# Tensor engine: sample rows' high and low parts as one stationary block in the down products, a 360-column last chunk, and an earlier start of the first up products

## What is computed

```python
mix = jnp.concatenate([o_b, o_a], axis=-1) @ w_out[l]
x = x + rmsnorm(mix, norm_mix_post[l])
f, new_buf = conv_ffn(rmsnorm(x, norm_ffn_pre[l]), conv_buf, w_up[l], conv_w[l], conv_b[l], w_down[l])
x = x + rmsnorm(f, norm_ffn_post[l])

def conv_ffn(xn, buf, w_up, conv_w, conv_b, w_down):
    h = xn @ w_up                                   # 1024 -> 2 * 2816
    hp = jnp.concatenate([buf, h], axis=1)
    c = conv_b + sum(conv_w[j] * hp[:, j:j + L] for j in range(3))
    g, u = jnp.split(c, 2, axis=-1)
    return (jax.nn.silu(g) * u) @ w_down, hp[:, L:]  # 2816 -> 1024
```

## Time and profile before

| | |
|---|---|
| time, median of 3 runs | 1434.85 us (1434.38 to 1435.5) |
| profiled execution, its time | 1435.23 us |
| profiled execution, span from first to last instruction | 1433.5 us |
| PE busy | 1390.9 us, 97% |
| DVE busy | 706.1 us, 49% |
| ACT busy | 464.0 us, 32% |
| POOL busy | 170.4 us, 12% |
| granted TensorE clock, mean | 0.993 |

### The profile page before, as it was taken

How to read it: one execution, slowest core, us unless ns; L and a number is a source line. 1 busy time by engine, 2 the same in 40 slices (tenths; PEclk the granted TensorE clock), 3 DMA queues, 4 the chain that set the end, 5 groups by cost and what they waited for, 6 DMA issues and landing times.

```text
span 1433.5 us, 22554 instructions
## 1 busy us (share of the span) xinstructions
PE 1390.9 (97%) x8818; PEld 1253.6 (87%) x8818; DVE 706.1 (49%) x1068; ACT 464.0 (32%) x779; POOL 170.4 (12%) x321
## 2 busy tenths in 40 slices
PE   7999999989999899999999999999999999999996
PEld 6999999957667688899898989898989898989995
DVE  5333322265666655445636353545454545353647
ACT  5421021065655544334132313132323232323233
POOL 2253000111222221120000000000000000000005
PEclk9999999999999999999999999999999999999998
DMA  7102022175573623132111101111110202020106
GB/s 256 60 30 63 30 96 74 66 211 171 161 223 117 192 87 118 66 96 74 30 59 29 59 29 59 29 48 40 32 55 16 71 15 73 15 73 15 45 23 129
DMA packets 93210, 112.39 MB, mean 78 GB/s; under 512 B 6413, under 2 KB 65206, under 8 KB 93142
## 3 DMA queue, kind: packets, MB, share of 16 engines
q1 hardware_dynamic: 89765, 103.34, 23.0%
q0 software_dynamic: 1136, 4.06, 1.6%
q10 hardware_dynamic: 2240, 4.06, 0.8%
HBM read 96.76 MB, written 14.69 MB: 78 GB/s over the span
## 4 chain that ended last, share of the span: by engine, by line
PE 89%; DVE 3%; issue 2%; ACT 2%; POOL 2%; DMA 1%; SPq 1%; ACTq 0%; DVEq 0%
PE PS L2086 36%; PE PS L2137 18%; PE PS L1821 16%; PE PS L2042 7%; PE PS L2156 2%; PE PS L1914 2%; PE PS L1983 1%; PE PS L1937 1%; PE PS L1882 1%; POOL small L1223 1%; DVE small L1412 1%; PE PS L1889 1%; PE PS L1904 1%; PE PS L1960 1%; PE PS L1807 1%
## 5 line engine op out<-in xcount | busy, mean ns | idle before, releaser
L2086 PE MATMUL PS<-act_hi,wu_hi 128*128 128x364 f32 x1056 | 347.7, 329 | 3.6 <-DVE wu_lo L1597 2.6
L2086 PE MATMUL PS<-act_lo,wu_hi 128*128 128x364 f32 x1056 | 347.7, 329 | 0.0
L2086 PE MATMUL PS<-act_hi,wu_lo 128*128 128x364 f32 x1056 | 347.5, 329 | 0.0
L2086 PEld LDWEIGHTS PS<-act_hi,wu_hi 128*128 128x128 f32 x1056 | 199.2, 189 | 4.3 <-DVE wu_lo L1597 2.7
L2086 PEld LDWEIGHTS PS<-act_lo,wu_hi 128*128 128x128 f32 x1056 | 199.0, 188 | 0.4
L2086 PEld LDWEIGHTS PS<-act_hi,wu_lo 128*128 128x128 f32 x1056 | 199.2, 189 | 0.0
L1649 DVE TENSOR_TENSOR y_acc<-y_acc,PS 128x512 f32<-128x512 f32 x180 | 123.3, 685 | 138.0 <-PE PS L2137 138.0
L2137 PE MATMUL PS<-wd_hi,g_hi 128*128 128x512 f32 x360 | 143.9, 400 | 0.0
L2137 PE MATMUL PS<-wd_hi,g_lo 128*128 128x512 f32 x360 | 142.3, 395 | 0.0
L2137 PE MATMUL PS<-wd_lo,g_hi 128*128 128x512 f32 x360 | 141.9, 394 | 0.0
L1110 ACT CAST g_hi<-conv 128x1088 fp32r<-128x1088 f32 x21 | 23.2, 1103 | 270.7 <-PE PS L2137 219.4
(11 more groups left out here) (254 smaller groups left out, 2335.7 us busy)
## 6 DMA issues: line engine op xcount, KB each, us to landing
wu_raw<-in_w_up_dram SPq DMA_DIRECT2D x44, 512.0 KB, 3.8
kpage<-in_cache_k_dram SPq DMA_DIRECT2D x64, 256.0 KB, 3.0
vpage<-in_cache_v_dram SPq DMA_DIRECT2D x64, 256.0 KB, 3.0
wd_raw<-in_w_down_dram SPq DMA_DIRECT2D x22, 512.0 KB, 5.3
w_raw<-in_w_in_dram SPq DMA_DIRECT2D x20, 512.0 KB, 4.8
wo_raw<-in_w_out_dram SPq DMA_DIRECT2D x8, 512.0 KB, 5.4
x_res<-in_x_prompt_dram SPq DMA_DIRECT2D x8, 512.0 KB, 4.3
out_dram<-x_mid SPq DMA_DIRECT2D x8, 512.0 KB, 2.9
```

The lines of the kernel that those rows point to most:

```text
L2086: mm = nc.tensor.matmul(PS[:, 3 * half + c, 0:CW], a[:, half, k, :], b[:, k, CHUNKS[c]], start=(j == 0), stop=(j == len(parts) - 1))
```

## The change

1. `g_hi` has 64 columns more. The product is cast into columns 64 to 1151; columns 0 to 63 take the sample rows' low part, written by an extra DVE instruction over 64 columns (`gs_lo_ready`). `g_lo` keeps the prompt only. For tile 8 the stationary block is columns 0 to 127 of `g_hi`, 64 low and 64 high parts of the same rows, and it is multiplied by `wd_hi` and by `wd_lo`: 4 matmuls in a group and not 6. The low parts' results gather in rows 64 to 127 of tile 8 of `y_acc`, to which all 128 rows are now added.
2. At the end these rows are moved to partitions 0 to 63 by a DMA on SP's queue (`y_fold`, 256 KB), behind a wait for the sample tile's two adds and ahead of the stores of the states; DVE adds them after the third tile's adds (`fold_sample`). Square, root, scaling and store of the sample tile come as the fourth (`NORM_POS`), and DVE makes two `final_norm` in the seventh step.
3. Chunk 2 is 360 columns wide in all up products, in the input projections u, k and q, and in the last copy.
4. The first up weights of both sides are split ahead of the last out tile's work (`wu_hi_first`, `wu_lo_first`), into the place of `w_out`'s high parts 0 to 3, behind a wait for the last tile's products that read them (`wo_used`). PE makes chunk 1 of the gate side right after the states, then turns tile 7 (into banks 4 and 5, which waits for the sample tile's `y_nrm`), makes chunk 2, turns the sample tile, and makes chunk 1 of the up side before it waits for the sample tile's split. `x2_hi` and `x2_lo` of tile 7 come after the sample tile's scaling.

```diff
-    g_hi = ffn.put("g_hi", [P, 2, NTOK], F32R)
-    g_lo = ffn.put("g_lo", [P, 2, NTOK], F32R)
+    g_hi = ffn.put("g_hi", [P, 2, NS + NTOK], F32R)
+    g_lo = ffn.put("g_lo", [P, 2, SEQ], F32R)
...
+    NORM_POS = [1, 2, 3, 0, 4, 5, 6, 7, 8]
+    y_fold = wd_raw[0:NS, 1, :]
...
         sp.dma_start(x_last, y_out[STEPS - 2]).then_inc(xlast_loaded, 16)
+        sp.wait_ge(ybank_free, YJ * (NIT - 1) + 2 + 2)
+        sp.dma_start(y_fold, y_acc[NS:P, STEPS - 1, :]).then_inc(fold_loaded, 16)
         for j, q in enumerate(STATES_FIRST):
             store_states(j, q)
...
         def wu_hi_first(half):
+            act.wait_ge(wo_used, 1)
...
+            if t == STEPS - 1:
+                wu_hi_first(0)
+                wu_hi_first(1)
             act.wait_ge(y_ready, t + 1)
...
             if t == STEPS - 1:
                 x2_hi(t - 2)
-                x2_hi(t - 1)
-                wu_hi_first(0)
...
-        wu_hi_first(1)
+        x2_hi(STEPS - 2)
         x2_hi(STEPS - 1)
...
             if t == STEPS - 1:
+                wu_lo_first(0)
+                wu_lo_first(1)
                 x2_lo(t - 2)
-                x2_lo(t - 1)
-                wu_lo_first(0)
             dve.wait_ge(yrstd_ready, t + 1)
...
-        wu_lo_first(1)
+        x2_lo(STEPS - 2)
         x2_lo(STEPS - 1)
+        for i in range(2):
+            dve.wait_ge(xmid_stored[i], 16 * ((STEPS + 1 - i) // 2))
...
-                    nc.vector.tensor_tensor(g_lo[:, e, :], conv[:, 1, :], g_hi[:, e, :].bitcast(F32), ALU.subtract).then_inc(g_lo_ready, 1)
+                    nc.vector.tensor_tensor(g_hi[:, e, 0:NS], conv[:, 1, 0:NS], g_hi[:, e, NS:2 * NS].bitcast(F32), ALU.subtract).then_inc(gs_lo_ready, 1)
+                    nc.vector.tensor_tensor(g_lo[:, e, :], conv[:, 1, NS:], g_hi[:, e, 2 * NS:].bitcast(F32), ALU.subtract).then_inc(g_lo_ready, 1)
...
         for t in range(STEPS):
             last_add(t, 0)
-            if t >= 2:
+            if 3 <= t <= 6:
+                final_norm(t - 3)
+            if t >= 6:
                 final_norm(t - 2)
             last_add(t, 1)
+            if t == 2:
+                fold_sample()
...
+            if t == STEPS - 2:
+                pe.wait_ge(ynrm_ready, STEPS)
...
-        pe.wait_ge(xt_lo_ready, 2 * STEPS + 2 * (STEPS - 1))
-        for c in (1, 2):
-            up_chunk(0, c)
+        pe.wait_ge(xt_lo_ready, 2 * STEPS + 2 * (STEPS - 3))
+        up_chunk(0, 1)
+        turn_x2(STEPS - 2)
+        up_chunk(0, 2)
         turn_x2(STEPS - 1)
+        pe.wait_ge(wu_lo_ready, 2)
+        pe.wait_ge(xt_lo_ready, 2 * STEPS + 2 * STEPS - 2)
+        up_chunk(1, 1)
         pe.wait_ge(xt_lo_ready, 2 * STEPS + 2 * STEPS)
...
-                for c in range(1 if first and t == 0 else 3):
+                for c in (0,) if first and t == 0 else (0, 2) if first and t == 1 else range(3):
                     mm = up_chunk(half, c)
...
+        def down_parts(s):
+
+            if s == STEPS - 1:
+                return [(g_hi[:, e, 0:2 * NS], w, e) for e in range(2) for w in (wd_hi, wd_lo)]
+            t = slice(2 * NS + P * s, 2 * NS + P * s + P)
+            return [(g, w, e) for e in range(2)
+                    for g, w in ((g_hi[:, e, t], wd_hi), (g_hi[:, e, t], wd_lo), (g_lo[:, e, P * s:P * s + P], wd_hi))]
```

More of the change, by code:

```diff
@@ L396, in _program, with kept @@
     KEPT = [slice(CW * c, min(CW * (c + 1), NTOK)) for c in range(3)]
+    def kept(c):
+        return KEPT[c].stop - KEPT[c].start
     jobs = []
@@ L1645, in add_down @@
             t, half = n // 2, n % 2
-            r = rows(t)
             dve.wait_ge(down_ready, base + n + 1)
-            dst = y_acc[0:r, t, 512 * half:512 * half + 512]
-            nc.vector.tensor_tensor(dst, dst, PS[0:r, 6 + half, :], ALU.add).then_inc(ybank_free, 1)
+            dst = y_acc[:, t, 512 * half:512 * half + 512]
+            nc.vector.tensor_tensor(dst, dst, PS[:, 6 + half, :], ALU.add).then_inc(ybank_free, 1)
         def ffn_dve(i, first, last):
@@ L1750, in last_add, with fold_sample @@
         def last_add(t, half):
-            s = LAST_TILES[t]
-            r, n = rows(s), 2 * t + half
+            s, n = LAST_TILES[t], 2 * t + half
             dve.wait_ge(down_ready, YJ * (NIT - 1) + n + 1)
-            dst = y_acc[0:r, s, 512 * half:512 * half + 512]
-            nc.vector.tensor_tensor(dst, dst, PS[0:r, LAST_BANK[t % 4] + half, :], ALU.add).then_inc(ybank_free, 1)
+            dst = y_acc[:, s, 512 * half:512 * half + 512]
+            nc.vector.tensor_tensor(dst, dst, PS[:, LAST_BANK[t % 4] + half, :], ALU.add).then_inc(ybank_free, 1)
+        def fold_sample():
+            dve.wait_ge(fold_loaded, 16)
+            dve.wait_ge(ybank_free, YJ * (NIT - 1) + 2 + 2)
+            dst = y_acc[0:NS, STEPS - 1, :]
+            nc.vector.tensor_tensor(dst, dst, y_fold, ALU.add).then_inc(fold_ready, 1)
         def final_norm(t, cs=slice(0, D)):
-            s = LAST_TILES[t]
+            s = LAST_TILES[NORM_POS[t]]
             r = rows(s)
@@ L1814, in project @@
                 else:
-                    out = PS[:, bank_of[n], 0:CW]
-                    pairs = [(w[:, g % 2, k, P * f:P * f + P], a[:, k, CHUNKS[c]]) for k in range(KD)
+                    out = PS[:, bank_of[n], 0:kept(c)]
+                    pairs = [(w[:, g % 2, k, P * f:P * f + P], a[:, k, KEPT[c]]) for k in range(KD)
                              for w, a in ((w_hi, act_hi), (w_hi, act_lo), (w_lo, act_hi))]
@@ L2058, in _ @@
                 mm = out_products(t, k, j == 0, j == KD - 1)
+                if t == STEPS - 1 and k in (1, 3):
+                    mm.then_inc(wo_used, 1)
             mm.then_inc(y_ready, 1)
@@ L2085, in up_chunk @@
             for j, (a, b, k) in enumerate(parts):
[L2086 removed]
+                mm = nc.tensor.matmul(PS[:, 3 * half + c, 0:kept(c)], a[:, half, k, :], b[:, k, KEPT[c]],
                                       start=(j == 0), stop=(j == len(parts) - 1))
@@ L2134, in down_share @@
                 pe.wait_ge(ybank_free, YJ * i + n + 1)
-                parts = [(g, w, e) for e in range(2) for g, w in ((g_hi, wd_hi), (g_hi, wd_lo), (g_lo, wd_hi))]
+                parts = down_parts(t)
                 for j, (g, w, e) in enumerate(parts):
-                    mm = nc.tensor.matmul(PS[:, 6 + half, :], g[:, e, wide(t)], w[:, e, 512 * half:512 * half + 512],
+                    mm = nc.tensor.matmul(PS[:, 6 + half, :], g, w[:, e, 512 * half:512 * half + 512],
                                           start=(j == 0), stop=(j == len(parts) - 1))
@@ L2153, in _ @@
                     pe.wait_ge(ybank_free, YJ * (NIT - 1) + 2 + 2 * (t - 4) + half + 1)
-                parts = [(g, w, e) for e in range(2) for g, w in ((g_hi, wd_hi), (g_hi, wd_lo), (g_lo, wd_hi))]
+                parts = down_parts(s)
                 for j, (g, w, e) in enumerate(parts):
-                    mm = nc.tensor.matmul(PS[:, LAST_BANK[t % 4] + half, :], g[:, e, wide(s)], w[:, e, 512 * half:512 * half + 512],
+                    mm = nc.tensor.matmul(PS[:, LAST_BANK[t % 4] + half, :], g, w[:, e, 512 * half:512 * half + 512],
                                           start=(j == 0), stop=(j == len(parts) - 1))
```

54 lines of the change are left out of this document (36 added, 18 removed).

## The result

The changed kernel takes **1421.75 us** (median of 4 runs, 1420.87 to 1422.97); the kernel before, on the same chip, 1434.84 (1434.38 to 1435.5, 4 runs). The ratio is 0.9909, 95% interval 0.9892 to 0.9926: 13.1 us less. That is 2.1 us above the forecast of 1419.6 and inside the wide range of 1417.0 to 1423.5, but 0.25 outside the forecast's own range of 1418.0 to 1421.5. The profiled execution took 1421.63 us, with a span of 1419.9.

A forecast was written before the change was run, and what follows sets the result against it. PE's own time was taken as the bound in the FFN. Shares 8.4, width 2.4 and transition 5.0 less closing stage 0.5 gave 15.3 us saved, so 1419.6 us; own range 1418.0 to 1421.5, wide range 1417.0 to 1423.5.

The forecast's parts named there:

- What bounds the kernel: FFN: PE's own time is the bound, 89% of the span; a matmul taken out counts in full unless something else comes last.
- 1. Shares: Ten down shares: four fewer matmuls each, 0.94 us less about 0.1 for a bank wait; net 8.4 us, between 7.0 and 9.4.
- Rival C: Down shares: the bank wait takes half of each share's gain, giving 1424 us; chance 0.06.
- rival E: Down shares: the new short PE wait brings the clock down, 18 us in ten shares, giving 1437.4 us; chance 0.01.
- 2. Width: Last chunks of up products and projections: 1344 matmuls with 4 columns less, 1.8 ns each; 2.4 us, range 0 to 2.5.
- Rival B: Last chunks: 360 columns cost what 364 do, giving 1422 us; chance 0.10.
- 3. Transition: First up products: 2.7 us idle, 1.8 of low clock, 1.15 idle go, 0.6 wait comes; gain 5.0, range 3.2 to 5.6.
- Rival A: Transition gives less: PE still idles, or the clock falls again at turns or the new wait; 1423 us, chance 0.12.
- 4. Closing stage: End of kernel: POOL's late root delays DVE's fifth scaling; end 0.5 us later though PE is 0.85 sooner, range -0.8 to +1.5.
- The sum: Whole kernel: 8.4 + 2.4 + 5.0 - 0.5 = 15.3 us saved, giving 1419.6 from the median of 1434.85.

The follow-up runs named there:

- e2: Kernel before with only the last chunk of up products and projections at 360 columns: 1432.65 us, ratio 0.9987.
- e1: Kernel before with only the new shares and closing stage, old width and old transition order: 1427.37 us, ratio 0.9947.
- e11: Kernel before plus unread identity transposes in PE's idle stretches ahead of the out products, no part of the change: 1434.53 us, ratio 1.0.
- e3: Kernel before with only the early split of the up weights and new order of turns and first up products: 1429.88 us, ratio 0.9965.
- e6: Changed kernel with POOL's closing root as one instruction, constant 1e-6 left out: 1420.75 us, ratio 0.9896.
- e4: The whole changed kernel once more, unaltered, in a later set of runs against the kernel before: 1420.17 us, ratio 0.99.
- e9: The whole changed kernel, unaltered, in another later set of runs against the kernel before: 1420.24 us, ratio 0.99.
- The fillers: Changed kernel plus identity transposes nobody reads, meant for PE's idle stretches ahead of and among the first out products: 1419.78 us, ratio 0.9898.
- e7: Changed kernel without the fold, sample tile first in the closing order, sample rows lacking their low parts' products: 1418.98 us in one execution.
- e12: Changed kernel without the fold and with the closing stage of before, now timed: 1418.40 us, ratio 0.9882.

## Why the prediction was right, and where it was not

**What bounds the kernel**: right. The share and the up products have moved by what their matmuls cost, and nothing else came last there.

**1. Shares**: right. Forecast 0.94 less 0.1 us each; measured 25.32 - 24.49 = 0.83. The cost is where it was laid out, at the second of the two short groups, whose load waits for the last add. Timelines of weight load and PE in after:

```profile
850.41 0.19 PEld L2195 LDWEIGHTS PS<-wd_hi,g_hi 128*128 128x128 f32 x1 [0.28 <-DVE y_acc L1677]
```

```profile
850.41 0.50 PE L2195 MATMUL PS<-wd_hi,g_hi 128*128 128x512 f32 x1
850.75 0.40 PE L2195 MATMUL PS<-wd_lo,g_hi 128*128 128x512 f32 x1
```

The step from one matmul to the next is 0.34 and not 0.234: 0.11 us, between the bounds of 0 and 0.24. Rival C (half the gain) is out, and so is the slower rival E: the nine iterations of after with that wait show no row of lower clock. What the Trainium skill ("TensorE: Matmul & The Clock Gate", A second HAM failure mode) tells of such small waits between PSUM banks, that the clock swings with them, did not happen here: this wait is 0.11 us of PE.

**2. Width**: the mechanism right, the size within 0.5 us. An up block of 288 has 96 narrower matmuls and takes 0.20 us less: 2.1 ns each, where 1.8 was forecast. Alone (e2) the part gave 1.95 us for a forecast of 2.4, with an interval of 0.6 to 3.2. Rival B (360 columns cost what 364 do) is out.

**3. Transition**: the right total, in part by luck, with one wrong reading. Measured from the start of the out products, the block of 288 begins at 634.63 - 511.38 = 123.25 us; before it was 128.19 by the prediction's reckoning. That is 4.94 sooner, forecast 5.0; the wait for the third low part is there:

```profile
633.44 1.15 DVE wu_lo L1691
634.63 48.02 PE PS L2131 x288
```

Rival A (the clock falls again at the turns, or a later split) is out: after has no row under 1.00 between 498 and 1409. But 1.8 of the 5.0 was the clock at 612, taken from one execution as if each had it. e1, e2 and e11 keep the idle stretch and don't show the fall, and by them it cost 1.5 to 1.6 and not 1.8 us (9.77 less 8.23 or 8.19); their transition takes 174.81, 174.57 and 174.85, and against them the early order saves 3.3 us (171.52 in e3) and not 4.9. That is what the three other terms of this part come to, 2.7 + 1.15 - 0.6. The 5.0 came out because the profile of before against which it is measured is the very execution with the fall, from which the forecast was worked out. The timed e3 gave 4.7, interval 3.2 to 6.7, which holds both. Its runs had a mean clock of 0.9948 and those of before beside them 0.9939, which by the line above is 0.7 of the 4.7 us, wherever it was lost. How often the timed runs of before lose the clock at 612 stays open. The term that was mis-sized is this one: the lower end of the part's range, 3.2, had been written down for the case that the clock falls in the new kernel; the case that it does not fall in the old one was missing.

**4. Closing stage**: the right number, +0.6 for +0.5, and half the wrong reason. The late root and DVE's wait of 0.73 are there, and cost the 1.1 us that e6 takes back. But PE's end was 1.28 sooner and not 0.85 (1.0 with the narrower products of the last pair), and DVE ended where it did before (56.47 against 56.55), not 0.4 to 0.5 later. The fold's transfer took 3.1 us, for 2.9 in the forecast, and DVE waited 0.19 us for it. The 0.6 came from the stores, at 6.2 for 5.5 us of queue, which the prediction had called "the same chain". The bound set there, that the last add trails PE's end by at most 2.5 us, holds: it starts at 1407.96, 1.2 us after PE's last product.

**The sum**: with the three parts as forecast, the first median still lay 2.1 us above. 1.6 us of it is found in the profiled execution ahead of the 96 out products, where 6.8 us of clock were lost and 3.4 in e4 and e9; the sum had no term for it. The three other runs of that set had a low mean clock too. The medians of e4 and e9 lay 0.6 us above the forecast. The own range, 1418.0 to 1421.5, took in this spread for the two later medians and missed the first by 0.25.

**A version that beats both** was not found. The fillers are 0.5 us under after on one chip, within the spread of both, and put in the right place they were not tried; the version without fold is 1.8 us under it, but leaves a part of the output out. An order that folds and yet issues its first store at 34.2 was not tried.

## What to carry to other kernels

Before you count a clock fall as a cost of an idle stretch, look at a second profile of the same kernel: here the 1.8 us counted from one execution were absent in three others that run the same code at that place. Where each timed run has its mean clock on record, read it beside the time: medians hide what it shows. Look in the timeline for where an added instruction really stands: transposes meant for an idle stretch stood behind it and cost 2.1 us, about what they were to bring. In a closing stage, follow the stores from the first issue and not only from the last instruction: where the DMA engines are full, a shorter chain on the compute engines only lengthens the queue (e6), and the two versions that started the first store 2.4 us sooner (e7, e12) are the ones that ended sooner. A matmul taken out of a chain that PE sets is worth its interval in full, less the wait for the bank of the group behind.

## What the runs showed of the hardware

The granted clock falls to 0.50, that is 1.2 GHz, behind idle stretches of PE in some executions and not behind the same stretches in others: at 612 in before, not in e1, e2 or e11, all of which are idle there for 2.59 us; at 463 in after, not in e4 or e9, which are the same kernel. Each fall costs 1.7 us of clock, or twice that. In the timed runs of one kernel, too, those with the higher mean clock are the shorter ones: e11 took 1432.0 to 1433.27 us at 0.998 and 1434.34 to 1437.78 at 0.994.

The DMA engines, at a share of 1.0, moved 190 to 230 GB/s of output stores while the end drew near, and a store's landing time grew from 6.0 to 7.4 us when the stores came up to 1.1 us sooner.

A GpSimd instruction on 128x1 elements took 0.19 us beside a DVE instruction with one input in PSUM, and 1.24 us beside one of 64x1024 with both inputs in SBUF.
